# Nine tile buffers in the key and value memory, and more accumulations taken along with each chunk behind the norms

## The chip, the cores and the metric

The kernel runs as one program on one core of one Trainium2 chip. The time is device microseconds (us) of one execution; the time before is the median of three runs. TensorE (PE) multiplies, VectorE (DVE) and ScalarE (ACT) work elementwise, GpSimd (POOL) splits weights, and SyncE (SP) issues most DMA transfers.

## The reference

Two decoder layers are applied to a prompt of 1024 tokens and to 8 sequences of 4 new tokens, 1056 token columns in all, with a model width of 1024. Cut to what matters:

```python
for layer in range(2):
    h = rms_norm(x, g_attn)
    qa, ka, va, qb, kb, vb = split(h @ w_in)      # per head: rms_norm and partial rotary on q and k
    oa = dilated_attention(qa, ka, va)            # 8 heads
    ob = window_attention(qb, kb, vb, sink)       # 8 query heads, 2 key and value heads
    x = x + concat(rms_norm(oa), rms_norm(ob)) @ w_out
    h = rms_norm(x, g_ffn)
    x = x + (silu(h @ w_gate) * (h @ w_up)) @ w_down
```

The new keys and values and the moved caches are outputs too. All is float32.

## The kernel before

The activations `xm` lie transposed: 8 chunks of 128 features by 1056 tokens. Every large product is made of three TensorE matmuls on rounded parts (high by high, low by high, high by low), in the helper `product` (L402). 1056 tokens are three pieces of 352 columns (`NW`, `W`), each in a PSUM bank of its own; `ps` has eight banks. One unit of 128 output features is 3 pieces x 8 chunks x 3 matmuls = 72 matmuls of 352 columns.

**Start and end.** SP loads the input in nine tiles (`x_load`, L415) into two buffers `xy_tile`; from the third tile on it waits until TensorE has transposed the tile two before (`x_tile_turned`). VectorE copies the transposed halves into `xm` (L927). All engines meet (`met`) and the layer loop begins. After the last layer TensorE transposes back (L1658), VectorE copies two halves per tile into the same two buffers (L1280), and SP stores them; a copy into a buffer waits for the store two tiles before (`y_tile_out`).

**Norms.** A norm squares and adds the chunks, takes roots, and spreads their reciprocals over the partitions by transposes into banks 5 to 7 (`spread_roots`, L1313). Then `norm_chunks` walks over the chunks: VectorE makes chunk c (`hf`, L953), ScalarE rounds it to the high part (L689), VectorE subtracts it for the low part of chunk c-1 (L958) and signals `lo_ready`. TensorE begins the next product chunk by chunk behind that signal. Between attention and the output projection there are two norms of four chunks each; the spread of the second stands in TensorE's order behind the fourth chunk's matmuls.

**Projection.** Units are numbered u: 0 is the key of the window heads, 1 their value, then for each of four pairs p key, query, query, value (u = 2+4p to 5+4p). Units alternate between banks 0 to 2 and 3 to 5. POOL splits the weights of unit u+2 (L588, L591) once unit u is `projected`. For keys and queries ScalarE squares the unit (`head_squares`, L702), TensorE sums by heads (`sum_heads`, L1338), ScalarE takes the roots by Ln and Exp (L708, L711), VectorE applies the rotary factors (`roped`). Keys and values are turned by TensorE through banks 6 and 7 (`turn`, L1346). `stage` is one buffer: value units are copied into it to be turned (`stage_v`, L717), and turned keys are kept in it (`keep_k`, L724) until a DMA has stored them (`k_out`).

**Output projection.** `out_unit(dd, i)` is unit 2dd+i, with its weights in `f_hi[i]`, `f_lo[i]`. SP loads the weights of unit 2 only behind the second reload of `xm` (`x_back`, L544), which waits for the eighth `hf` chunk; POOL then splits them.

**Feed-forward.** A step f makes six hidden pieces (k = 0 to 5, each 48 matmuls: gate and up), and then 24 downward products of 6 matmuls. Piece k waits until piece k-2 has been multiplied by its gate (`gated`): ScalarE's Silu (L897), then VectorE's product (L1261).

The order of instructions on each engine is that of the code; nothing plans it at build time.

## Time and profile before

| what | value |
|---|---|
| median of three runs | 3042.84 us (3041.46 to 3046.21) |
| the profiled execution | 3039.55 us |
| its span | 3038.0 us |
| busy: PE, DVE, ACT, POOL | 2839.4, 1175.8, 915.5, 507.5 us |
| chain that ended last, by engine | PE 89%, DVE 5%, issue 3%, ACT 2%, DMA 1% |
| share of the chain on the product helper L402 | 68% |

The span is what the trace covers; 1.55 us of the execution lie around it. Each row of a timeline gives the start, the duration (a merged row gives the time that it covers), the engine and its line, what is written and read, the shape and the count, and in brackets the idle time before it and what ended that.

### The profile page before, as it was taken

Reading aid. Unit: us, or ns where it says so; the run is one execution under the profiler, and the core shown is the slowest. Engines: PE = TensorE matmul, PEld = TensorE weight load, DVE = VectorE, ACT = ScalarE, POOL = GpSimd, SP = SyncE. Lnnn points to the kernel's source line nnn. Section 1 sums busy time; section 2 is a strip of 40 time slices with the busy share of each in tenths; the row PEclk is TensorE's granted clock in tenths of the full one; section 3 lists DMA queues with packets and bytes.
Section 4 is the critical chain, followed back from the end, with each engine's and each line's share of the span. In section 5 each row is a group of like instructions: output and inputs, shape, how many; then the busy total and the mean of one; then the engine's idle time right before and its main releaser. Section 6 shows DMA issues by size and latency. Waiting matters only on the chain.

```text
span 3038.0 us, 51313 instructions
## 1 busy us (share of the span) xinstructions
PE 2839.4 (93%) x19000; PEld 2612.0 (86%) x19000; DVE 1175.8 (39%) x2420; ACT 915.5 (30%) x1662; POOL 507.5 (17%) x211
## 2 busy tenths in 40 slices
PE   4999899878999999999969999997889999999998
PEld 3999666578999999999959986665879999999998
DVE  5445555453322222222254455554442222322223
ACT  2334665521211111121033446654121111211110
POOL 1222000022111221122022210001212111221110
PEclk6999999978999999999979999998989999999999
DMA  4121533132555454411021244321344544454111
GB/s 160 43 63 49 169 103 104 50 99 83 182 181 181 155 175 159 153 41 52 3 94 49 63 114 130 107 77 40 99 154 159 176 153 153 153 181 140 41 41 57
DMA packets 182629, 333.35 MB, mean 110 GB/s; under 512 B 30352, under 2 KB 142096, under 8 KB 179664
## 3 DMA queue, kind: packets, MB, share of 16 engines
q1 hardware_dynamic: 171632, 195.26, 21.0%
q0 software_dynamic: 2816, 135.99, 13.4%
q8 instruction: 87, 1.43, 0.2%
q10 hardware_dynamic: 8032, 0.17, 0.2%
q14 instruction: 62, 0.51, 0.1%
HBM read 309.15 MB, written 157.94 MB: 154 GB/s over the span
## 4 chain that ended last, share of the span: by engine, by line
PE 89%; DVE 5%; issue 3%; ACT 2%; DMA 1%; DVEq 0%; ACTq 0%; SPq 0%
PE ps L402 68%; PE ps L1415 4%; PE ps L1429 3%; PE ps L1404 3%; PE ps L1338 2%; PE ps L1478 1%; DVE g_lo L958 1%; PE ps L1466 1%; PE ps L1447 1%; DVE t_buf L943 1%; PE ps L1303 1%; DVE hf L953 1%; PE ps L1454 1%; DVE hf L943 1%; DMA kt_all<-in_x_prompt_dram 1%
## 5 line engine op out<-in xcount | busy, mean ns | idle before, releaser
L402 PE MATMUL ps<-g_hi,f_hi 128*128 128x352 f32 x2496 | 816.0, 327 | 33.2 <-DVE g_lo L958 33.2
L402 PE MATMUL ps<-g_hi,f_lo 128*128 128x352 f32 x2496 | 811.9, 325 | 0.0
L402 PE MATMUL ps<-g_lo,f_hi 128*128 128x352 f32 x2496 | 810.6, 325 | 0.0
L402 PEld LDWEIGHTS ps<-g_hi,f_hi 128*128 128x128 f32 x2496 | 475.0, 190 | 39.8 <-DVE g_lo L958 39.8
L627 POOL TENSOR_TENSOR f_lo<-f_raw,f_hi 128x2048 fp32r<-128x2048 f32 x66 | 303.9, 4618 | 1197.0 <-ACT f_hi L875 1197.0
L402 PEld LDWEIGHTS ps<-g_lo,f_hi 128*128 128x128 f32 x2496 | 476.1, 191 | 0.0
L402 PEld LDWEIGHTS ps<-g_hi,f_lo 128*128 128x128 f32 x2496 | 475.9, 191 | 0.0
L1261 DVE TENSOR_TENSOR silu<-silu,ps 128x352 f32<-128x352 f32 x132 | 68.8, 521 | 821.1 <-ACT silu L897 821.1
L1271 DVE TENSOR_TENSOR xm<-xm,ps 128x352 f32<-128x352 f32 x528 | 270.9, 520 | 199.7 <-PE ps L402 199.7
L402 PE MATMUL ps<-a_hi,f_hi 128*128 128x352 f32 x1056 | 340.7, 323 | 0.0
L402 PE MATMUL ps<-a_hi,f_lo 128*128 128x352 f32 x1056 | 338.5, 321 | 0.0
L402 PE MATMUL ps<-a_lo,f_hi 128*128 128x352 f32 x1056 | 338.3, 320 | 0.0
L402 PE MATMUL ps<-h_hi,w_hi 128*128 128x352 f32 x864 | 289.6, 335 | 14.4 <-DVE h_lo L958 14.4
L402 PE MATMUL ps<-h_lo,w_hi 128*128 128x352 f32 x864 | 278.6, 323 | 0.0
L402 PE MATMUL ps<-h_hi,w_lo 128*128 128x352 f32 x864 | 278.6, 322 | 0.0
L897 ACT ACTIVATE silu<-ps 128x352 f32<-128x352 f32 x132 | 61.3, 465 | 653.5 <-PE ps L402 653.3
L763 ACT ACTIVATE pt<-ps 128x512 f32<-128x512 f32 (+3 forms) x320 | 133.4, 437 | 216.5 <-PE ps L1415 215.9
L402 PEld LDWEIGHTS ps<-a_hi,f_lo 128*128 128x128 f32 x1056 | 198.4, 188 | 0.0
L402 PEld LDWEIGHTS ps<-a_hi,f_hi 128*128 128x128 f32 x1056 | 198.1, 188 | 0.0
L402 PEld LDWEIGHTS ps<-a_lo,f_hi 128*128 128x128 f32 x1056 | 197.9, 187 | 0.0
L402 PEld LDWEIGHTS ps<-h_hi,w_hi 128*128 128x128 f32 x864 | 163.5, 189 | 20.2 <-DVE h_lo L958 17.3
L402 PEld LDWEIGHTS ps<-h_hi,w_lo 128*128 128x128 f32 x864 | 164.0, 190 | 2.8
(164 smaller groups left out, 3337.2 us busy)
## 6 DMA issues: line engine op xcount, KB each, us to landing
out_dram<-in_cache_a_dram POOLq DMA_DIRECT2D x16, 8176.0 KB, 27.1
f_raw<-in_w_gate_up_dram SPq DMA_DIRECT2D x44, 1024.0 KB, 6.3
f_raw<-in_w_down_dram SPq DMA_DIRECT2D x22, 1024.0 KB, 5.0
k_near<-in_cache_a_dram SPq DMA_DIRECT2D x16, 1024.0 KB
v_near<-in_cache_a_dram SPq DMA_DIRECT2D x16, 1024.0 KB
w_raw<-in_w_in_dram SPq DMA_DIRECT2D x28, 512.0 KB, 3.9
k_far<-in_cache_a_dram SPq DMA_DIRECT2D x16, 768.0 KB
v_far<-in_cache_a_dram SPq DMA_DIRECT2D x16, 768.0 KB
```

Of the source, the lines that this page charges most:

```text
L402: mm = pe.matmul(out, left(a, c), right(b, c), start=(start and c == 0 and k == 0), stop=(stop and c == n - 1 and k == 2))
L627: nc.gpsimd.tensor_tensor(f_lo[j][:], f_raw[j % 2][:], f_hi[j][:].bitcast(F32), ALU.subtract).then_inc(f_split.sem, 1)
L763: nc.scalar.activation(pt[:, g % 4, 0:(b - a) * P], ps[:, 3 + g % 2, 0:(b - a) * P], ACT.Copy).then_inc(pt_ready.sem, 1)
L897: nc.scalar.activation(silu[:, k % 2, :], ps[:, 2 * (k % 2), 0:W], ACT.Silu).then_inc(silued.sem, 1)
L943: nc.vector.tensor_tensor(acc[:, 0:T], acc[:, 0:T], sq[:, 0:T], ALU.add).then_inc(sq_added.sem, 1)
L953: nc.vector.scalar_tensor_tensor(hf[c % 2][:], xm[:, first + c, :], gains[:, gain + first + c:gain + first + c + 1], flat(bank), ALU.mult, ...
L1261: nc.vector.tensor_tensor(silu[:, k % 2, :], silu[:, k % 2, :], ps[:, 2 * (k % 2) + 1, 0:W], ALU.mult).then_inc(gated.sem, 1)
L1271: nc.vector.tensor_tensor(xs, xs, ps[:, 4 + (n * DC + d) % 4, 0:W], ALU.add).then_inc(ffn_added.sem, 1)
L1338: mm = pe.matmul(ps[:, bank + c, 0:W], blocks[:], t_buf[1][:, c * W:(c + 1) * W], start=True, stop=True)
L1404: pe.matmul(ps[:, k % 3, 0:w], xm[half, p + (NP if m == "b" else 0), i * P:(i + 1) * P], kt_all[half, 1 + p if m == "a" else 0, first:firs ...
L1415: mm = pe.transpose(ps[:, 3 + g % 2, (c - a) * P:(c - a + 1) * P], probs_of(d, hh)[:, c * P:(c + 1) * P], ident[:])
L1429: mm = pe.matmul(ps[half, 5, 0:P], v_all[:, 1 + p if m == "a" else 0, tiles[c], half], pt[:, g % 4, (c % 4) * P:(c % 4 + 1) * P], start=(c ...
```

## The change

1. `xy_tile` has nine buffers, made of the five key planes and four of the value planes. All nine loads are issued at once, ahead of the six constants. The waits on `x_tile_turned` in SP and on `y_tile_out` in VectorE go.
2. Behind the first norm of a layer TensorE takes with each chunk three pieces of unit 0 and two of unit 1 (15 matmuls instead of 9); unit 1's third piece follows by itself. It waits for both splits first. The order behind it changes for p = 0: the window value is staged before the roots of the window key, and turned before that key is. All banks of the units behind it are exchanged (0 to 2 with 3 to 5), and those of attention too.
3. The same behind the norms ahead of the output projection: three pieces of unit 0 and two of unit 1 with each chunk.
4. Behind the feed-forward norm the chunks take hidden pieces 0 and 1 together (12 matmuls instead of 6). Step f = 0 is written out ahead of the loop.

```diff
-        xy_tile = [kt_all[:, 2 + i, 0:SEQ] for i in range(2)]
+        xy_tile = [kt_all[:, i, 0:SEQ] for i in range(1 + NP)] + [v_all[:, i].rearrange("p j n -> p (j n)") for i in range(NP)]
@@ SP
-            x_load(0)
-            x_load(1)
+            for t in range(QT + 1):
+                x_load(t)
...
-            for t in range(2, QT + 1):
-                sp.wait_ge(x_tile_turned, 2 * (t - 1))
-                x_load(t)
@@ ACT
                 nc.scalar.activation(pieces(t_buf[1][:, 0:T]), banks(0), ACT.Square).then_inc(head_sq.sem, 1)
+                stage_v(1, 0)
                 roots_of_heads(0, 0)
-                keep_k(0, kv_rows[:, 0, NP, :])
+                keep_k(0, 2, kv_rows[:, 0, NP, :])
...
-                stage_v(1, 0)
@@ DVE, the output
-                if t >= 2:
-                    dve.wait_ge(y_tile_out[t % 2], 16 * (t // 2))
@@ PE, behind the first norm
-                pe.wait_ge(w_split.sem, w_split.at(l, 1))
+                pe.wait_ge(w_split.sem, w_split.at(l, 2))
                 for c in range(DC):
                     pe.wait_ge(lo_ready.sem, lo_ready.at(l, c + 1))
-                    for n in range(NW):
+                    for u, n in ((0, 0), (0, 1), (0, 2), (1, 0), (1, 1)):
...
-                project(1, 1, 3, (0,))
+                project(1, 1, 3, (2,))
                 sum_heads(0, 0, 0)
-                project(1, 1, 3, (1, 2))
...
                     if p == 0:
+                        pe.wait_ge(v_staged.sem, v_staged.at(l, 1))
+                        project(u, 0, 3, (0,))
+                        turn(stage, 5, v_turned)
+                        project(u, 0, 3, (1,))
+                        pe.wait_ge(v_kept.sem, v_kept.at(l, 3))
+                        project(u, 0, 3, (2,))
                         pe.wait_ge(rope.sem, rope.at(l, r))
                         turn(kt_all[:, 0, :], 2, k_turned)
+                        project(u + 1, 1, 0, (0,))
+                        sum_heads(3, h, r)
@@ PE, the output projection
-                pe.wait_ge(o_split.sem, o_split.at(l, 1))
+                pe.wait_ge(o_split.sem, o_split.at(l, 2))
                 for c in range(DC):
                     if c == NP:
                         pe.wait_ge(hf_ready.sem, hf_ready.at(l, 12))
                         spread_roots(l, 2, 5)
                     pe.wait_ge(lo_ready.sem, lo_ready.at(l, 8 + c + 1))
-                    for n in range(NW):
+                    for i, n in ((0, 0), (0, 1), (0, 2), (1, 0), (1, 1)):
...
+                product(pe, ps[:, 5, 0:W], lambda a, c: (f_hi, f_lo)[a][1][:, D + c * P:D + (c + 1) * P],
+                        lambda a, c: (g_hi, g_lo)[a][:, c, 2 * W:3 * W], DC).then_inc(o_done[1].sem, 1)
...
-                out_unit(0, 1)
@@ PE, the feed-forward
+                pe.wait_ge(f_split.sem, f_split.at(l, 2))
+                for c in range(DC):
+                    pe.wait_ge(lo_ready.sem, lo_ready.at(l, 16 + c + 1))
+                    for k in range(2):
+                        mm = hidden_chunk(k, c)
+                        if c == DC - 1:
+                            mm.then_inc(hid.sem, 1)
+                for k in range(2, HID):
+                    hidden_piece(0, k)
+                down_pieces(0)
+                with pe.Fori(1, FI) as f:
```

SP's queue at the start of the program; `kt_all` and `v_all` hold the tile buffers.

```order
 L417 DMA ident<-in_c_ident_dram 128x128
-L415 DMA kt_all<-in_x_prompt_dram 128x1024 x2
+L415 DMA kt_all<-in_x_prompt_dram 128x1024 x5
+L415 DMA v_all<-in_x_prompt_dram 128x1024 x3
+L415 DMA v_all<-in_x_sample_dram 32x1024
 L422 DMA ones<-in_c_ones_dram 128x1
 L422 DMA blocks<-in_c_blocks_dram 128x128
```

Seven of the nine loads move ahead of the constants, and nothing waits between them.

ScalarE behind the first norm of a layer, before: the squares of the key unit (L732), its roots (L708, L711), the turned key kept (L724, L727), its store, and then the value staged (L717).

```order
L732 ACTIVATE t_buf<-ps 128x1056
L707 ISA
L708 ACT_TABLE_LOAD
L708 ACTIVATE t_buf<-ps,eps 128x1056
L710 ISA
L711 ACT_TABLE_LOAD
L711 ACTIVATE t_buf<-t_buf 128x1056
```

```order
L727 ACTIVATE kv_rows<-ps 32x128
L736 ISA
L736 DMA out_dram<-stage 128x128
L715 REGISTER_ALU
L716 ISA
L717 ACTIVATE stage<-ps 128x1056
```

The same place of the changed kernel:

```order
L731 ACTIVATE t_buf<-ps 128x1056
L711 REGISTER_ALU
L714 ACTIVATE stage<-ps 128x1056
L703 ISA
L704 ACT_TABLE_LOAD
L704 ACTIVATE t_buf<-ps,eps 128x1056
```

The staging copy (L717 before, L714 now) has moved from behind the store of the kept key to behind the squares.

TensorE at the first chunk behind the feed-forward norm, before; `f_hi0` is the gate's weights and `f_hi1` those of up.

```order
L402 MATMUL ps<-g_hi,f_hi0 128x352
L402 MATMUL ps<-g_hi,f_lo0 128x352
L402 MATMUL ps<-g_lo,f_hi0 128x352
L402 MATMUL ps<-g_hi,f_hi1 128x352
L402 MATMUL ps<-g_hi,f_lo1 128x352
L402 MATMUL ps<-g_lo,f_hi1 128x352
L1634 REGISTER_ALU
```

And now, from the same place to the next chunk's wait:

```order
L1310 MATMUL ps<-ident,roots 128x32
L1663 ISA
L1665 REGISTER_ALU
L402 MATMUL ps<-g_hi,f_hi0 128x352
L402 MATMUL ps<-g_hi,f_lo0 128x352
L402 MATMUL ps<-g_lo,f_hi0 128x352
L402 MATMUL ps<-g_hi,f_hi1 128x352
L402 MATMUL ps<-g_hi,f_lo1 128x352
L402 MATMUL ps<-g_lo,f_hi1 128x352
L402 MATMUL ps<-g_hi,f_hi0 128x352
L402 MATMUL ps<-g_hi,f_lo0 128x352
L402 MATMUL ps<-g_lo,f_hi0 128x352
```

The six matmuls of piece 0 are followed by six of piece 1 (three are shown) before TensorE waits for the next chunk.

## Rows read from the trace of the kernel before

**Rows 1.** Timeline of the start of the program (start, duration, engine, operation).

```profile
10.76 3.25 ACTq L662 DMA_DIRECT2D gains_all<-in_ffn_norm_dram  x1
...
20.61 1.43 ACTq L664 DMA_DIRECT2D sinks_all<-in_sinks_b_dram  x1
...
33.56 1.28 ACT L675 ACT_TABLE_LOAD   x1 [33.56 <-DVEq L962]
```

**Rows 2.** The DMA view of the stretch from 9 to 12 us.

```profile
DMA packets 687, 1.19 MB, mean 396 GB/s; under 512 B 388, under 2 KB 407, under 8 KB 687
```

**Rows 3.** Timeline behind layer 0's first norm.

```profile
59.84 0.66 PE L402 MATMUL ps<-h_hi,w_hi 128*128 128x352 f32 x1 [3.82 <-DVE h_lo L958]
...
60.30 0.50 PE L402 MATMUL ps<-h_hi,w_lo 128*128 128x352 f32 x1
...
60.59 0.49 PE L402 MATMUL ps<-h_lo,w_hi 128*128 128x352 f32 x1
...
65.10 0.32 PE L402 MATMUL ps<-h_hi,w_hi 128*128 128x352 f32 x1
...
73.64 2.49 DVE L958 TENSOR_TENSOR h_lo<-kt_all,h_hi 128x1056 fp32r<-128x1056 f32 x2
```

**Rows 4.** The chain that ended last, in order of time (start, duration, what).

```profile
81.88 1.77 PE ps L1338 x6
...
109.93 1.77 PE ps L1338 x6
...
1603.29 1.77 PE ps L1338 x6
...
2262.79 753.89 PE ps L402 x4716
```

**Rows 5.** Timeline of TensorE behind layer 1's first norm.

```profile
1553.25 0.66 PE L402 MATMUL ps<-h_hi,w_hi 128*128 128x352 f32 x1 [3.81 <-DVE h_lo L958]
...
1556.58 0.33 PE L402 MATMUL ps<-h_lo,w_hi 128*128 128x352 f32 x1
```

**Rows 6.** Timelines of DVE, SP and POOL at layer 0's output projection.

```profile
645.54 2.54 DVE L953 SCALAR_TENSOR_TENSOR hf<-xm,gains,ps 128x1056 f32<-128x1056 f32 x2 [3.44 <-PE ps L1313]
...
669.56 1.25 DVE L1241 TENSOR_TENSOR xm<-xm,ps 128x1056 f32<-128x1056 f32 x1 [10.19 <-PE ps L402]
...
639.66 13.91 SPq L544 DMA_DIRECT2D xm<-x_spill  x2
...
664.62 2.40 POOL L591 TENSOR_TENSOR f_lo<-f_raw,f_hi 128x1024 fp32r<-128x1024 f32 x1 [0.18 <-POOL f_hi L588]
```

**Rows 7.** The same of layer 1: TensorE, POOL and VectorE.

```profile
2138.03 1.20 PE L1313 MATMUL ps<-ident,roots 128*128 128x128 f32 x9
...
2158.90 2.40 POOL L591 TENSOR_TENSOR f_lo<-f_raw,f_hi 128x1024 fp32r<-128x1024 f32 x1 [0.18 <-POOL f_hi L588]
...
2162.87 1.25 DVE L1241 TENSOR_TENSOR xm<-xm,ps 128x1056 f32<-128x1056 f32 x1 [10.34 <-PE ps L402]
```

**Rows 8.** Timelines at the first hidden pieces of both layers: TensorE's seventh chunk, ScalarE.

```profile
769.45 0.66 PE L402 MATMUL ps<-g_hi,f_hi 128*128 128x352 f32 x1 [0.39 <-DVE g_lo L958]
...
772.63 1.28 ACT L897 ACT_TABLE_LOAD   x1 [3.28 <-PE ps L402]
...
775.14 0.50 ACT L901 ACTIVATE a_hi<-silu 128x352 fp32r<-128x352 f32 x1 [0.75 <-DVE silu L1261]
...
780.23 0.46 ACT L897 ACTIVATE silu<-ps 128x352 f32<-128x352 f32 x1 [4.59 <-PE ps L402]
...
2274.28 0.46 ACT L897 ACTIVATE silu<-ps 128x352 f32<-128x352 f32 x1 [4.67 <-PE ps L402]
```

**Rows 9.** Timeline of VectorE in the output stage.

```profile
3018.36 2.48 DVE L1280 COPY kt_all<-ps 128x512 f32<-128x512 f32 x4 [1.14 <-PE ps L1658]
...
3034.30 1.28 DVE L1280 COPY kt_all<-ps 32x512 f32<-32x512 f32 x2 [1.42 <-DMA out_dram<-kt_all]
```

**Rows 10.** The DMA view from 3018 to 3024 us: GB/s in forty equal slices.

```profile
GB/s 0 0 0 0 0 109 0 0 0 0 0 0 0 0 0 0 27 410 410 437 437 410 410 410 355 383 437 437 410 410 328 410 410 437 28 0 0 0 0 0
```

More of the change, by code:

```diff
@@ L225, in trunk @@
         eps_set = sem("eps_set")
-        x_tile_in = [sem(f"x_tile_in{i}") for i in range(2)]
+        x_tile_in = [sem(f"x_tile_in{i}") for i in range(QT + 1)]
         x_tile_turned = sem("x_tile_turned")
@@ L230, in trunk @@
         y_tile_kept = sem("y_tile_kept")
-        y_tile_out = [sem(f"y_tile_out{i}") for i in range(2)]
+        y_tile_out = sem("y_tile_out")
         met = sem("met")
@@ L715, in stage_v, with keep_k @@
                     act.wait_ge(projected.sem, projected.at(l, unit + 1))
-                    act.wait_ge(k_out.sem, k_out.at(l, 16 * (n + 1)))
-                    nc.scalar.activation(pieces(stage[:]), banks(3), ACT.Copy).then_inc(v_staged.sem, 1)
-                def keep_k(n, rows):
-                    act.wait_ge(v_turned.sem, v_turned.at(l, 3 * n))
+                    if n >= 1:
+                        act.wait_ge(k_out.sem, k_out.at(l, 16 * (n + 1)))
+                    nc.scalar.activation(pieces(stage[:]), banks(0 if n else 3), ACT.Copy).then_inc(v_staged.sem, 1)
+                def keep_k(n, bank, rows):
+                    act.wait_ge(v_turned.sem, v_turned.at(l, 3 * max(n, 1)))
+                    if n == 1:
+                        act.wait_ge(k_out.sem, k_out.at(l, 16))
                     for g in range(2):
@@ L992, in roped, with k_rope @@
                     dve.wait_ge(rope.sem, rope.at(l, r + 5))
-                def k_rope(unit, gain, r, root, kt):
-                    roped(unit, 0, gain, 1.0, r, root)
+                def k_rope(unit, bank, gain, r, root, kt):
+                    roped(unit, bank, gain, 1.0, r, root)
                     nc.vector.tensor_tensor(kt, t_buf[0][:], t_buf[1][:, 0:T], ALU.mult).then_inc(rope.sem, 1)
@@ L1007, in q_rope, with keep_v @@
                                                 ALU.mult).then_inc(rope.sem, 1)
-                def keep_v(n, v, rows):
+                def keep_v(n, bank, v, rows):
                     for g in range(2):
@@ L1377, in _ @@
-                    project(u + 1, 1, 3, (1,))
-                    pe.wait_ge(v_kept.sem, v_kept.at(l, 3 * p + 3))
-                    project(u + 1, 1, 3, (2,))
+                        project(u + 1, 1, 0, (0,))
+                        sum_heads(3, h, r)
+                        project(u + 1, 1, 0, (1,))
+                        pe.wait_ge(k_kept.sem, k_kept.at(l, 3))
+                        project(u + 1, 1, 0, (2,))
+                    else:
+                        pe.wait_ge(head_root.sem, head_root.at(l, 2 * h - 1))
+                        project(u, 0, 3, (0, 1))
+                        pe.wait_ge(v_staged.sem, v_staged.at(l, p + 1))
+                        turn(stage, 2, v_turned)
+                        project(u, 0, 3, (2,))
+                        project(u + 1, 1, 0, (0,))
+                        sum_heads(3, h, r)
+                        project(u + 1, 1, 0, (1,))
+                        pe.wait_ge(v_kept.sem, v_kept.at(l, 3 * p + 3))
+                        project(u + 1, 1, 0, (2,))
@@ L1392, in _ @@
+                    project(u + 3, 1, 0, (1, 2))
                 pe.wait_ge(rope.sem, rope.at(l, K_ROPE + NP * ROPE_P))
@@ L1428, in mix @@
                             g = groups_of[d, hh][c // 4]
-                            mm = pe.matmul(ps[half, 5, 0:P], v_all[:, 1 + p if m == "a" else 0, tiles[c], half],
+                            mm = pe.matmul(ps[half, 2, 0:P], v_all[:, 1 + p if m == "a" else 0, tiles[c], half],
                                            pt[:, g % 4, (c % 4) * P:(c % 4 + 1) * P],
@@ L1650, in _ @@
                                     ).then_inc(downed.sem, 1)
+                pe.wait_ge(f_split.sem, f_split.at(l, 2))
+                for c in range(DC):
+                    pe.wait_ge(lo_ready.sem, lo_ready.at(l, 16 + c + 1))
+                    for k in range(2):
+                        mm = hidden_chunk(k, c)
+                        if c == DC - 1:
+                            mm.then_inc(hid.sem, 1)
+                for k in range(2, HID):
+                    hidden_piece(0, k)
+                down_pieces(0)
+                with pe.Fori(1, FI) as f:
+                    pe.wait_ge(f_split.sem, f_split.at(l, 3 * f + 2))
+                    for k in range(HID):
+                        hidden_piece(f, k)
+                    down_pieces(f)
                 meet(pe, l, 1)
```

116 lines of the change are left out of this document (52 added, 64 removed).

## The prediction

> **What bounds the kernel now.** The chain of waits, in order of time, comes first: apart from the norms, the start and the end it is an unbroken line of matmuls, the last of them 4716 in 753.89 us, 0.160 us each [rows 4]. Work taken off another engine is worth nothing there; TensorE has to begin work earlier in a place where it waits. Those places are read from the timelines: the start, where the layer's first instruction waits until 33.56 [rows 1]; behind each norm, where VectorE delivers a chunk every 2.51 us (first chunk 59.84, seventh at the end of the first of the two subtractions, 73.64 + 1.25 = 74.9: 15.05 over 6) [rows 3]; the output, where copies wait for stores [rows 9]. TensorE's matmuls start 0.29 us apart at first (60.30, 60.59) and last 0.32 instead of 0.50 from 65.10 on [rows 3], with starts 0.16 apart; 352 columns in 0.29 us is the 1.2 GHz level, in 0.16 about the 2.4 GHz level.
>
> **Start.** The loads of tiles 2 to 8 no longer wait for transposes and stand ahead of the constants. 4.3 MB of tiles at the 396 GB/s of [rows 2] are 11 us; begun at about 4 us, with the small gain transfers between, the last lands near 18, and two copies (about 0.65 each) per tile keep up: all is kept by 20 or 21. But the layer also waits until ScalarE has issued its gain loads. That ended at 20.61 + 1.43 = 22.0, and a single issue took 3.25 us while SP's transfers filled the engines [rows 1, 2]. SP now keeps them full to about 20 or 21 (6.2 MB), 4 or 5 us longer without a break, so I let the slow issues last 2.7 us more: 24.7. Layer start 33.4 to 24.7: **8.7 us gained**. Bounds: 12 if issuing is not slowed and the tiles decide, 3 if every issue is slow. I take 8.7, nearest to the rows.
>
> **Behind the first norm, twice.** 15 matmuls need 15 x 0.16 = 2.4 us at the upper clock, just under the chunk's 2.51; at the lower one 15 x 0.293 = 4.4. Layer 0: from 59.84 to the rise at 64.8 TensorE does 17; the other 103 follow without a gap, 16.4 us: 81.2 (never waiting, since data alone would allow 79.8). Then unit 1's last piece, 24 x 0.159 = 3.8: 85.0; summing by heads 1.77 [rows 4]: 86.8. Staging of the value runs under it (ScalarE's copy of three banks, about 1.1 from 85.1). Then unit 2's pieces 3 x 3.8, two turns of 1.2 and one piece of unit 3, 3.8: the next head sum starts at 104.5 instead of 109.93 [rows 4]: 5.5 gained. Layer 1: start 1553.25, upper clock from 1556.4 (the 0.33 of 1556.58) [rows 5], 11 done by then, 109 x 0.159: 1573.8; the same steps (23.3 us) give 1597.1 instead of 1603.29 [rows 4]: 6.2. **Together 11.7.** The second split is waited for too; TensorE's wait for the first chunk was ended by VectorE [rows 3, 5], and POOL had by then long finished both, so it costs nothing. One new tightness: the key kept in `stage`, with its store's issue, now stands right ahead of the squares of unit 2; by the same durations the squares and VectorE's first product are ready within 0.3 us of the head sum. If that cover goes, about 1 us per layer. Later pairs keep their order with other banks: zero.
>
> **Output projection, twice.** Here the gain turns round. The second norm's spread stands behind the fourth chunk's matmuls, which are now 60, not 36. In layer 0 the 24 more go at the upper clock, 3.8 us, and VectorE's fifth chunk starts at 645.54 + 3.8 [rows 6]. In layer 1 TensorE had idled 0.8 us among the four chunks before the spread at 2138.03 [rows 7], as the clock had risen sooner; that idle is filled first, and the spread comes 3.0 later, at 2141.0. The second reload of `xm` waits for the eighth chunk (the pair of issues ends at 639.66 + 13.91 = 653.57 [rows 6]), the weights of unit 2 are queued behind it on SP, and POOL's split ended at 664.62 + 2.40 = 667.0, and at 2158.90 + 2.40 = 2161.3 [rows 6, 7]. All of that moves with the spread: 670.8 and 2164.3. TensorE began unit 2 when unit 1 was done, 669.4 and 2162.7 (VectorE's additions at 669.56 and 2162.87, less 0.15) [rows 6, 7]. By its own work it would now be there at 668.9 and 2161.1: fifth chunk ready at 653.1 and 2146.1, 60 matmuls with it and the next three and 24 behind them, the first 19 and 16 of these at the lower clock. So it waits for the split: 1.4 and 1.6 later than before. **3.0 lost.** The ends: if the reload or the load behind it is quicker than before by the delay, 2.0 gained; if the lower clock holds over all of the first four chunks, 60 x 0.293 puts the spread 9 us late and the loss is 6.6 per layer.
>
> **Feed-forward norm, twice.** 12 matmuls are 1.9 us at the upper clock, so the chunks still set the pace; the backlog of the first, slow ones is caught up. Seventh chunk at 769.45 [rows 8] and 2262.79 [rows 4]; 24 x 0.159 + 0.1 for both last chunks: pieces 0 and 1 are done at 773.4 and 2266.7. But piece 2 needs piece 0 gated. Piece 0 ends 0.95 earlier, and from its end to the gate took 772.63 to 775.14, 2.5 us, with the table load of 1.28 inside, behind the wait [rows 8]. So piece 2 starts at 775.1 and 2268.4, with 1.7 us of idle TensorE where before the 48 matmuls of piece 1 hid this. Before it started at 780.1 and 2274.15 (second Silu less 0.13) [rows 8]. **5.0 + 5.8 = 10.8 gained.** If the table load were done ahead, 2.5 more; if a chunk's matmuls fell back to the lower clock near the end, 3.5 less.
>
> **Output.** The copies run free: 2.48 / 4 = 0.62 each [rows 9]. The sample tile is kept at 3018.36 + 18 x 0.64 = 3029.9 instead of 3034.30 + 1.28 = 3035.6. Stores of 0.52 MB at the 410 GB/s of the full stretches take 1.28 us each [rows 10], as long as two copies, so they trail by up to 0.5: **5.2 gained** (4.3 to 5.8). The Trainium skill has a lower limit (DMA: Bandwidth & Descriptors, "Where 436 GB/s comes from"): about 358 GB/s bind between HBM and SBUF. By it a store takes 1.46 us and eight of them end 1.4 us later, a gain of 3.8 here and a sum of 1.4 less; the rows show 410 to 437, though only for 2.6 us at a stretch, so for a long burst they leave it open.
>
> **Sum.** 8.7 + 11.7 - 3.0 + 10.8 + 5.2 = 33.4. The profiled execution took 3039.55, which gives 3006.2; the median of the runs was 3.3 above it, so 3009.5.
>
> The page on ScalarE's tables prices the switch of tables higher (the Trainium skill, ScalarE: Activation LUTs, "What ACT_TABLE_LOAD costs": about 2.66 us with a drain). Here the load is 1.28 and the Silu starts right behind it, inside the measured 2.5 [rows 8]; by the page each layer's wait would be 1.4 longer, 2.8 in all.
>
> **Rivals.**
> - *Gains at the start don't come.* The tiles arrive early, but ScalarE's issues are starved for as long as SP's transfers run: 3 instead of 8.7 gained, 3015. For it speaks the 3.25 us issue [rows 1]; against it, that most issues before it were far shorter.
> - *The projection's split is not late.* The reload's wait shifts, but the weights arrive in less time: 5 better, 3004.5. Against it stands the unbroken chain on SP [rows 6].
> - *Stores at a slower rate.* In a burst of 10 us instead of 2.6 the stores keep the 355 GB/s of a slow slice [rows 10], 1.48 us each, and the copies no longer set the pace: 1.6 less gained, 3011. For it: no stretch of full length was there before; against it: most slices show 410. (The page's limit named above would do the same.)
> - *The other side: the lower clock stays through the chunk loops.* Then every 15 matmuls take 4.4 us against 2.51, and the loops are TensorE's: 120 x 0.293 = 35.2 us instead of about 21 puts the first norm 8.3 us behind before instead of 6 ahead, per layer; the output projection loses 10 to 11 per layer, the feed-forward norm 3.5 to 4. That is 46 lost against 14 gained at start and end: 3042 + 32 = 3074. It decides if the clock does not rise in more than about half of the six loops. Against it: it rose with only 9 matmuls per chunk, within 5.0 and 3.2 us of the first one [rows 3, 5], and the loops are denser now.
> - *Not what it says:* a wait in front of an early chunk (second split, `v_staged`) cancels the overlap and the norms give nothing; start and end alone leave 3039.55 - 13.9 + 3.3 = 3029.
>
> **How the numbers follow.** Forecast 0.60, start 0.14, split not late 0.10, slower stores 0.08, overlap cancelled 0.04, clock 0.04. Each of the first four has some 4 us of its own, since the moment at which the clock rises differs between runs by about 2 us per loop. The range from 3001 to 3021 takes in those four. About 0.2% (6 us) is what a measurement here can tell. Faster 0.95, same 0.02, slower 0.03.
>
> **What would show it.** Right: the first table load near 25 us; the head sum of unit 2 20 us behind unit 0's, without idle ahead of it; VectorE's fifth chunk at the output projection 3 to 4 us later behind the first; TensorE idle ahead of unit 2, ended by POOL; 1.5 to 2 us idle ahead of piece 2, ended by VectorE; copies of the output in one run. Wrong: matmuls of 0.50 us in the second half of any chunk loop, idle of VectorE between chunks, or a layer start after 30 us.

## The result, and the profile after

The changed kernel took 3018.18 us, median of 4 runs (3009.97 to 3023.77); the kernel before 3042.40 beside it (3041.46 to 3046.21, 4 runs). The ratio is 0.9917, 95% interval 0.9904 to 0.9930: faster by 0.8%. The profiled execution is the fastest of the four, 3009.97, span 3008.4, which is 29.6 less than the 3038.0 of before. The traces are compared stage by stage, so the parts below add up to 29.6, and not to the 24 between the medians; the section on the prediction says where the difference between the two comes from.

The start. Timeline of the changed kernel, start and duration in us:

```profile
12.53 7.18 ACTq L658 DMA_DIRECT2D gains_all<-in_ffn_norm_dram  x1
...
12.79 7.23 DVE L926 COPY xm<-ps 128x512 f32<-128x512 f32 x13 [0.16 <-PE ps L1291]
...
25.76 0.53 ACTq L660 DMA_DIRECT2D sinks_all<-in_sinks_b_dram  x1
...
26.69 1.28 ACT L671 ACT_TABLE_LOAD   x1 [26.69 <-ACTq L687]
```

The tiles are kept at 12.79 + 7.23 = 20.0. The layer starts at 26.69, because ScalarE has to issue its gain loads first; one of them occupied its queue for 7.18 us. The corresponding row of before shows 3.25, and the layer began at 33.56, behind the tiles [rows 1].

Behind layer 0's first norm, timeline of the changed kernel:

```profile
52.95 0.66 PE L402 MATMUL ps<-h_hi,w_hi 128*128 128x352 f32 x1 [3.81 <-DVE h_lo L957]
...
94.88 1.05 ACT L698 ACTIVATE t_buf<-ps 128x1056 f32<-128x1056 f32 x1 [0.76 <-ACT kv_rows L726]
...
95.97 1.32 DVE L980 TENSOR_SCALAR t_buf<-ps,gains 128x1056 f32<-128x1056 f32 x1 [8.29 <-ACT t_buf L698]
...
97.34 2.04 PE L1335 MATMUL ps<-t_buf,blocks 128*128 128x352 f32 x6
```

and the head sum of unit 2 in the kernel before, in the same view:

```profile
109.77 1.94 PE L1338 MATMUL ps<-t_buf,blocks 128*128 128x352 f32 x6
```

From the first chunk's matmul to unit 2's head sum are 97.34 - 52.95 = 44.39 us; before they were 109.77 - 59.84 = 49.93 [rows 3]. (The chain in [rows 4] has that head sum 0.16 later, at 109.93, so the two views must not be mixed.) The head sum starts as soon as VectorE's product ends (95.97 + 1.32 = 97.29). That product waits for ScalarE's squares, and those wait 0.76 behind the key that ScalarE keeps (`kv_rows`).

The output projection, TensorE, POOL and SP of the changed kernel:

```profile
627.75 16.54 SPq L541 DMA_DIRECT2D xm<-x_spill  x2
...
635.02 1.20 PE L1310 MATMUL ps<-ident,roots 128*128 128x128 f32 x9
...
644.85 0.39 SPq L529 DMA_DIRECT2D f_raw<-in_w_out_dram  x1
...
654.55 1.04 POOL L584 CAST f_hi<-f_raw 128x1024 fp32r<-128x1024 f32 x1 [38.65 <-DMA f_raw<-in_w_out_dram]
...
655.76 2.35 POOL L587 TENSOR_TENSOR f_lo<-f_raw,f_hi 128x1024 fp32r<-128x1024 f32 x1 [0.18 <-POOL f_hi L584]
...
658.30 0.66 PE L402 MATMUL ps<-g_hi,f_hi 128*128 128x352 f32 x1 [3.03 <-POOL f_lo L587]
...
660.81 0.49 PE L402 MATMUL ps<-g_lo,f_hi 128*128 128x352 f32 x1
...
2143.12 0.66 PE L402 MATMUL ps<-g_hi,f_hi 128*128 128x352 f32 x1 [3.02 <-POOL f_lo L587]
```

Read it from the last wait backwards. TensorE is idle for 3.03 us in layer 0 and 3.02 in layer 1, until POOL has split unit 2's weights. POOL had waited for their load. The load was issued at 644.85, right behind the reload of `xm`, whose pair of issues ends at 627.75 + 16.54 = 644.29. Behind the wait the matmuls take 0.49 again, as at the start of a chunk loop. A window of 3 us shows it as a granted clock. Columns are the window, its length, busy time and number of instructions of PE, PEld, DVE, ACT, POOL, then the granted clock, the DMA share and GB/s. First the kernel before, which needed no wait there:

```profile
658.00:661.00 3.00, 3.00 (x21) 3.00 (x20) 1.26 (x1) 1.09 (x1) 0.00 (x0) 1.00 0.96 361
```

and the changed kernel, where the first matmuls of unit 2 ran at half clock, the 1.2 GHz level:

```profile
658.00:661.00 3.00, 2.70 (x9) 2.71 (x10) 1.23 (x1) 0.00 (x0) 2.82 (x3) 0.50 0.39 110
```

Behind the feed-forward norm, ScalarE and TensorE of the changed kernel:

```profile
762.93 1.28 ACT L896 ACT_TABLE_LOAD   x1 [3.34 <-PE ps L402]
...
765.30 0.43 PE L402 MATMUL ps<-g_hi,f_hi 128*128 128x352 f32 x1 [1.52 <-DVE silu L1260]
765.44 0.50 ACT L900 ACTIVATE a_hi<-silu 128x352 fp32r<-128x352 f32 x1 [0.75 <-DVE silu L1260]
...
773.27 0.47 ACT L896 ACTIVATE silu<-ps 128x352 f32<-128x352 f32 x1 [4.00 <-PE ps L402]
```

TensorE waits 1.52 us in front of piece 2, ended by VectorE's gate. From the table load to the kept gated piece are 765.44 - 762.93 = 2.51 us, exactly as before, 775.14 - 772.63 [rows 8]; but 48 matmuls no longer hide them.

The output, VectorE and SP of the changed kernel:

```profile
2994.44 6.07 DVE L1277 COPY kt_all<-ps 128x512 f32<-128x512 f32 x10 [1.14 <-PE ps L1685]
...
2995.76 5.12 SPq L571 DMA_DIRECT2D out_dram<-kt_all  x5
...
3000.43 4.85 DVE L1277 COPY v_all<-ps 128x512 f32<-128x512 f32 x8
...
3001.73 3.91 SPq L571 DMA_DIRECT2D out_dram<-v_all  x4
```

The copies run through, 0.61 us each, where the last one of before had waited until 3034.30 [rows 9]. The stores follow at their pace, as the DMA view from 2996 to 3008 shows (GB/s in forty slices of 0.3 us, and the sums):

```profile
GB/s 0 0 410 410 410 396 423 382 396 423 396 423 396 423 355 423 423 382 437 396 423 355 423 369 437 410 423 382 396 410 423 410 396 423 396 382 355 300 0 0
...
DMA packets 1200, 4.33 MB, mean 360 GB/s; under 512 B 144, under 2 KB 144, under 8 KB 1200
```

### The profile page after: what moved, and what is told of

Same layout as the page of the kernel before. It is cut to its first block, busy times and chain, and to the rows that moved or that the text cites. A ratio compares the mean times of both kernels' runs of the same rounds, so it can differ in the third digit from the quotient of the medians.

```text
span 3008.4 us, 51127 instructions
## 1 busy us (share of the span) xinstructions
PE 2827.9 (94%) x19000; PEld 2607.7 (87%) x19000; DVE 1171.7 (39%) x2420; ACT 916.4 (30%) x1662; POOL 510.6 (17%) x211
## 4 chain that ended last, share of the span: by engine, by line
PE 89%; DVE 4%; issue 2%; ACT 2%; ACTq 1%; DMA 1%; POOL 0%; SPq 0%; DVEq 0%; POOLq 0%
PE ps L402 69%; PE ps L1422 4%; PE ps L1436 4%; PE ps L1411 3%; PE ps L1335 2%; PE ps L1485 1%; PE ps L1473 1%; DVE g_lo L957 1%; PE ps L1454 1%; DVE t_buf L942 1%; PE ps L1300 1%; DVE hf L952 1%; PE ps L1461 1%; DVE hf L942 1%; ACT pt L762 1%
## 5 line engine op out<-in xcount | busy, mean ns | idle before, releaser
L402 PEld LDWEIGHTS ps<-g_hi,f_hi 128*128 128x128 f32 x2496 | 473.8, 190 | 38.9 <-DVE g_lo L957 28.7
L402 PEld LDWEIGHTS ps<-h_hi,w_hi 128*128 128x128 f32 x864 | 163.5, 189 | 10.8 <-DVE h_lo L957 7.9
```

The source lines that it names most:

```text
L402: mm = pe.matmul(out, left(a, c), right(b, c), start=(start and c == 0 and k == 0), stop=(stop and c == n - 1 and k == 2))
```

## The experiments

Medians are of the runs of each kernel; every ratio is to the kernel before on the same chip. The groups ran on different chips, so kernels of different groups are compared by their ratios. In the text "stretch" is the time from the output norms' first chunk to the feed-forward norm's first sum of squares in the trace of the one profiled execution: 110.4 and 109.5 us in layers 0 and 1 of the kernel before, 112.7 and 112.8 in the changed one.

| kernel | median us (range, runs) | ratio, 95% interval |
|---|---|---|
| nine buffers alone | 3033.01 (3027.77 to 3035.76, 6) | 0.9967, 0.9955 to 0.9980 |
| first norm alone | 3030.18 (3029.00 to 3031.73, 5) | 0.9964, 0.9950 to 0.9978 |
| output projection alone | 3053.17 (3046.86 to 3056.45, 7) | 1.0030, 1.0018 to 1.0041 |
| feed-forward norm alone | 3033.98 (3028.60 to 3039.34, 10) | 0.9967, 0.9957 to 0.9977 |
| changed kernel again | 3016.66 (3009.31 to 3024.25, 4) | 0.9900, 0.9877 to 0.9923 |
| all but the output projection | 3010.91 (3007.05 to 3014.16, 4) | 0.9887, 0.9869 to 0.9904 |
| weights ahead of the reloads | 3011.09 (3006.47 to 3017.64, 4) | 0.9889, 0.9867 to 0.9912 |
| that, and the wait filled | 2996.39 (2991.47 to 2998.17, 4) | 0.9836, 0.9820 to 0.9853 |
| table load ahead | 3009.39 (3008.00 to 3012.35, 4) | 0.9884, 0.9868 to 0.9901 |
| constants late | 3014.12 (3011.28 to 3020.91, 4) | 0.9902, 0.9881 to 0.9923 |
| wait filled and table ahead | 2994.45 (2993.13 to 2997.26, 4) | 0.9834, 0.9818 to 0.9851 |
| that, and constants late | 2993.96 (2991.86 to 2995.69, 4) | 0.9832, 0.9816 to 0.9849 |

The first four share 19 runs of the kernel before (median 3043.89), the next four 7 (3042.20), the last four 7 (3045.95).

### The four parts alone

Only the buffers and their waits at start and end (the parts of the diff at `xy_tile`, `x_load` and the output):

```diff
-        xy_tile = [kt_all[:, 2 + i, 0:SEQ] for i in range(2)]
+        xy_tile = [kt_all[:, i, 0:SEQ] for i in range(1 + NP)] + [v_all[:, i].rearrange("p j n -> p (j n)") for i in range(NP)]
```

> Only the nine tile buffers (all loads issued at once, no waits for stores). Theory (each part acts by itself, as the two traces show it): layer start at about 27 instead of 33.6 us, output stage 5.7 us shorter, 12.6 us faster in all; the layer start is set by ScalarE's issue of its gain loads, with single issues of 3 to 7 us. Rival (the start's gain is an accident of one execution, with ScalarE's issues free to take longer in others): 6 us or less, and the timed runs spread over more than 5 us. Rival (the spread of the changed kernel's runs, 3010 to 3024, comes from elsewhere): these runs lie within 5 us of each other, as those of before.

Measured: ratio 0.9967, about 10 us (6 to 14 by the interval). The layer starts at 26.56; in every kernel with this part and the constants in their old place it is 26.56 to 26.76, so the start is not what scatters. The six runs lie 8 us apart, and not within 5.

Only the first norm (15 matmuls per chunk and the other banks behind it):

```diff
-                    for n in range(NW):
+                    for u, n in ((0, 0), (0, 1), (0, 2), (1, 0), (1, 1)):
```

> Only 15 matmuls per chunk behind the first norm of each layer, with the new order for p = 0 and the exchanged banks. Theory: 5.7 us per layer, 11.4 faster, head sum of unit 2 at about 104.2 instead of 109.9 us. Rival (the exchanged banks cost something in attention): from the head sum of unit 2 to the end of attention more than the 495 to 498 us of before in both layers, and less than 8 us gained.

Measured: ratio 0.9964, about 11 us. From the first chunk's start on VectorE to unit 2's head sum are 48.3 and 47.9 us, against 53.7 in both layers before. The rival, a cost of the exchanged banks in attention, is not seen: from that head sum to the output norms' first chunk are 525.0 and 525.3 us, where kernels with the old banks have 522.2 to 529.1.

Only the output projection:

```diff
-                    for n in range(NW):
+                    for i, n in ((0, 0), (0, 1), (0, 2), (1, 0), (1, 1)):
```

> Only 15 matmuls per chunk behind the norms ahead of the output projection. Theory (late spread, late reload, late weights, and a fall of the clock in the wait): 5.6 us slower, TensorE idle about 3 us ahead of unit 2 with POOL as the releaser, in both layers. Rival (the part saves 36 matmuls per layer as the other norms do): 8 to 11 us faster.

Measured: ratio 1.0030 with the interval above 1, so this part alone makes the kernel slower, by 5 to 12 us. The stretch is 112.8 and 113.6. TensorE in this kernel, ahead of unit 2 in the two layers:

```profile
671.98 0.66 PE L402 MATMUL ps<-g_hi,f_hi 128*128 128x352 f32 x1 [2.80 <-POOL f_lo L591]
...
2175.92 0.43 PE L402 MATMUL ps<-g_hi,f_hi 128*128 128x352 f32 x1 [1.82 <-POOL f_lo L591]
...
2176.97 0.48 PE L402 MATMUL ps<-g_hi,f_hi 128*128 128x352 f32 x1
```

The idle of about 3 us was expected in both layers; the second had 1.82, and even that was followed by matmuls of 0.48, one microsecond later.

Only the feed-forward norm (pieces 0 and 1 taken along with every chunk):

```diff
+                for c in range(DC):
+                    pe.wait_ge(lo_ready.sem, lo_ready.at(l, 16 + c + 1))
+                    for k in range(2):
+                        mm = hidden_chunk(k, c)
```

> Only the two hidden pieces taken along behind the feed-forward norm. Theory: 5.2 and 5.9 us in the two layers, 11.1 faster, with 1.5 us of idle TensorE ahead of piece 2 ended by VectorE's gate product. Rival (the wait for the gate takes the most of it back): under 6 us.

Measured: ratio 0.9967, about 10 us, with 1.52 us of idle ahead of piece 2 in both layers. From the norm's first chunk to the third Silu are 33.8 us in both layers, against 38.7 and 39.4 before. The four ratios add up to -0.72%; for the whole change -0.83% and -1.00% were measured in two comparisons. The parts are additive within their intervals.

### Where the output projection loses

The changed kernel again, as a base for the next comparisons:

> The changed kernel once more, to stand beside the three kernels of this group. Theory (the four parts add up: 12.6 + 11.4 + 11.1 gained, about 7 lost at the output projection by the segments of the traces): 28 faster than before in the middle, single runs within about 5 us of it as in the kernel before. Rival (its runs really spread more than those of before, because the start or the clock is less steady): single runs over 10 us apart, and the profile shows where against the first one.

Measured: 0.9900, 3009.31 to 3024.25. The expectation that single runs lie within about 5 us of the middle failed: they span 15 us. The kernel before is not steady to 5 us either; its 19 runs beside the four parts span 3038.58 to 3051.95. The profiled execution here was the slowest of the four, 3024.25, which serves below to find the scatter.

The change without its output projection:

```diff
-                    for i, n in ((0, 0), (0, 1), (0, 2), (1, 0), (1, 1)):
+                    for n in range(NW):
```

> The changed kernel without its part at the output projection (9 matmuls per chunk there, unit 1 behind, as before). Theory: that part costs 3 to 4 us per layer, so this is 7 us faster than the changed kernel; from the first chunk of the output norms to the sum of the next norm 109.4 us in both layers instead of 112.8. Rival (the loss seen when the part stood alone, 9 us with an interval of 5 to 12, was that of its runs): within 3 us of the changed kernel.

Measured: 3010.91, with a stretch of 109.7 and 110.5. Without that part the changed kernel is better, 5.7 by the medians of this comparison; the ranges of runs overlap, and the traces (2.3 to 3.0 per layer) say the same.

The theory that the load of unit 2's weights is late because it is queued behind the reloads on SP. Both units' weights are issued first:

```diff
+                for i in range(2):
+                    sp.wait_ge(o_split.sem, o_split.at(l, i + 1))
+                    sp.sem_inc(waits_alone, 1)
+                    o_load(i, 2 + i)
                 for i in range(2):
                     sp.wait_ge(hf_ready.sem, hf_ready.at(l, 12 + 4 * i))
...
-                with sp.Fori(1, DC // 2) as dd:
+                with sp.Fori(2, DC // 2) as dd:
```

> The changed kernel, but SP loads the output projection's weights of units 2 and 3 ahead of both reloads of xm instead of behind them. Theory (what costs there is that the weights stand behind the late reload): TensorE's 3.0 us of idle ahead of unit 2 are gone and the clock doesn't fall, 108 us for the stretch instead of 112.8, 4.7 us per layer, 9 faster than the changed kernel. Rival (the late spread itself is what costs, or the reload is needed as early): the stretch keeps 111 us or more.

Measured: 3011.09, stretch 109.8 and 109.5, where 108 was expected. VectorE and POOL of this kernel:

```profile
643.28 2.54 DVE L956 SCALAR_TENSOR_TENSOR hf<-xm,gains,ps 128x1056 f32<-128x1056 f32 x2 [6.93 <-PE ps L1314]
...
658.69 1.04 POOL L588 CAST f_hi<-f_raw 128x1024 fp32r<-128x1024 f32 x1 [39.94 <-PE ps L402]
```

POOL now waits for TensorE to leave the old weights, and no longer for a DMA; there is no idle time ahead of unit 2. So the late split was the queue on SP. But VectorE still waits 6.93 us for the spread: the first half of the step is unchanged, and the gain of the 24 added matmuls does not arrive. TensorE of this kernel at its fifth chunk, and the window behind it:

```profile
647.06 0.66 PE L402 MATMUL ps<-g_hi,f_hi 128*128 128x352 f32 x1 [3.81 <-DVE g_lo L961]
...
645.00:652.00 7.00, 4.94 (x17) 4.94 (x18) 6.93 (x6) 3.96 (x4) 0.00 (x0) 0.53 0.09 17
```

TensorE is idle for 3.81 us there, as it was in the kernel before and in the changed one (3.8 in each layer), and the granted clock of the window is 0.53. The clock does fall in this kernel, at the fifth chunk, which the expectation of 108 had left out.

Then the same work is put where TensorE waits, behind the spread instead of in front of it:

```diff
                     if c == NP:
                         pe.wait_ge(hf_ready.sem, hf_ready.at(l, 12))
                         spread_roots(l, 2, 5)
+                        for x in range(NP):
+                            for n in range(2):
+                                out_piece(1, n, x)
                     pe.wait_ge(lo_ready.sem, lo_ready.at(l, 8 + c + 1))
                     for i, n in ((0, 0), (0, 1), (0, 2), (1, 0), (1, 1)):
+                        if i == 1 and c < NP:
+                            continue
```

> As the one before, and the second norm's spread isn't late either: with the first four chunks TensorE takes only unit 0; behind the spread, where it had idled 3.8 us for the fifth chunk, it takes unit 1's 24 matmuls of those four chunks, and with chunks five to eight all 15. Theory: another 3.8 us per layer, the stretch is 104 to 105 us, 16 us faster than the changed kernel. Rival (the lower clock eats it: the 24 matmuls run at 0.29 us and the fifth chunk waits): 107 us or more.

Measured: 2996.39, stretch 103.8 and 103.7. TensorE and VectorE of this kernel, and a window behind the spread:

```profile
637.68 1.20 PE L1314 MATMUL ps<-ident,roots 128*128 128x128 f32 x9
638.82 0.43 PE L402 MATMUL ps<-g_hi,f_hi 128*128 128x352 f32 x1
638.92 2.54 DVE L956 SCALAR_TENSOR_TENSOR hf<-xm,gains,ps 128x1056 f32<-128x1056 f32 x2 [3.08 <-PE ps L1314]
...
638.00:652.00 14.00, 14.00 (x89) 13.44 (x88) 10.07 (x9) 4.35 (x4) 0.00 (x0) 1.00 0.46 175
```

VectorE starts its fifth chunk after 3.08 us of waiting instead of 6.93, and TensorE goes on at 638.82 with unit 1's matmuls for the first four chunks, without idle. The granted clock stays at 1.00. Each layer gains 8.9 to 9.1 against the changed kernel; 2.9 to 3.3 of it are the weights, issued first, and 6.0 and 5.9 are the filled wait. That is more than the 3.8 expected for the wait alone, and the rest fits the fall of the clock behind it, which is gone as well. Against the kernel before, the output projection now gains 6.6 and 5.8 us, where the changed kernel lost 2.3 and 3.3. The filling was tried only with the weights ahead.

### The table load, the start, and all together

```diff
                 norm_hi(l, 3, hf2, g_hi)
+                nc.scalar.activation(warm[:], eps[:, 0:1], ACT.Silu)
```

A Silu of one column into a tensor of its own, so that the table is loaded ahead of the wait.

> The changed kernel with one more ScalarE instruction: a Silu of a single column into a tensor of its own, behind the last rounding of the feed-forward norm, so that the table is loaded while chunks still come. Theory (the load of 1.28 us stands inside TensorE's wait for the gate): the idle ahead of hidden piece 2 falls from 1.52 to about 0.2 us in both layers, 2.6 us in all, less than the runs' own spread can tell but plain in the profile. Rival (the wait is VectorE's and ScalarE's passes, or the table is loaded a second time at the real Silu): 1.5 us stays.

Measured: 3009.39. ScalarE and TensorE of this kernel:

```profile
760.97 1.28 ACT L892 ACT_TABLE_LOAD   x1
...
764.32 0.47 ACT L898 ACTIVATE silu<-ps 128x352 f32<-128x352 f32 x1 [1.85 <-PE ps L403]
...
765.40 0.43 PE L403 MATMUL ps<-g_hi,f_hi 128*128 128x352 f32 x1 [0.25 <-DVE silu L1262]
```

The wait in front of piece 2 shrinks from 1.52 to 0.25, and from the first chunk to the third Silu are 32.5 and 32.4 us instead of 33.7: 1.3 per layer, the length of the load. (By ratios, 0.9884 against 0.9900 and 0.9917, it is 5 to 10 us faster than the changed kernel; the intervals overlap in the one comparison and nearly in the other, and no trace ties more than 2.6 of it to the table.)

```diff
             for t in range(QT + 1):
                 x_load(t)
+            sp.wait_ge(x_tile_kept, 2 * (QT + 1))
             for dst, src in ((ones, c_ones), (blocks, c_blocks), (cos, c_cos),
                              (sin, c_sin), (mask_a, c_mask_a), (mask_b, c_mask_b)):
                 sp.dma_start(dst[:], src).then_inc(consts_in, 16)
-            sp.wait_ge(x_tile_kept, 2 * (QT + 1))
```

> The changed kernel, but SP issues the six constants only when all input tiles are kept (about 20 us) and so leaves the DMA engines free between. Theory (ScalarE's gain loads are starved while SP's transfers run, 7.2 us for one issue): that issue ends about 4 us earlier and the layer starts at 22 to 24 us instead of 26.6. Rival (the 7744 elements of the gains, moved at some 760 per us, set the time, whatever SP does): layer start at 26 us or later, or later still.

Measured: 3014.12. The start in this kernel:

```profile
12.38 4.94 ACTq L658 DMA_DIRECT2D gains_all<-in_ffn_norm_dram  x1
20.93 0.53 ACTq L660 DMA_DIRECT2D sinks_all<-in_sinks_b_dram  x1
22.57 1.75 SPq L423 DMA_DIRECT2D mask_b<-in_c_mask_b_dram  x1
24.65 1.28 ACT L671 ACT_TABLE_LOAD   x1 [24.65 <-SPq L424]
```

With less traffic from SP, ScalarE has issued everything at 21.5 instead of 26.3, so it was SP's transfers that slowed it. The gain is in two issues: the one of 7.18 ends 2.4 earlier (about 4 were expected), and the next one, which in the changed kernel lasted 3.28 us beside the constants, lasts 0.78. Now SP itself ends the wait, since it issues the constants last: the layer starts 2.0 earlier, at 24.65, and not at 22 to 24. The comparison of runs is too coarse for so small a step.

The filled wait with the table load ahead, and then the constants late as well:

> The kernel with the weights first, the wait filled behind the second norm's spread, and the table loaded ahead, all on top of the change. Theory (the parts add up): 16 + 2.6 us faster than the changed kernel, 2994 us, and faster than both. Rival (the earlier steps push the squares of a layer against GpSimd's splits, whose overlap makes VectorE's additions take 3.2 instead of 1.27 us): 2998 or more.

> As c1_all, with the constants late too. Theory: another 3 to 4 us, about 2991, if the layer start moves to 22 to 24 us. Rival (the constants now stand ahead of the first weights in SP's queue, and the second split comes too late for the first chunk): no gain, with TensorE's first chunk behind POOL instead of VectorE.

Measured: 2994.45 and 2993.96. These beat the kernel before by 1.7% and, by ratios, the changed kernel by 20 to 25 us. The sum expected of the first, 2994, came; the further 3 to 4 us of the second did not. The layer starts at 23.05 in the last of them, and TensorE's first chunk is still ended by VectorE, so its rival is not what took the gain. Its distance from the one before it (1.7 in the spans, 0.5 in the medians) is not resolved by the runs. Nor is what the table load adds to the filled wait (0.9834 against 0.9836); in the trace it is the same 1.3 per layer.

## Why the prediction was right, step by step

The forecast was 3006.2 for a profiled execution and 3009.5 for the median, range 3001 to 3021. Measured were 3009.97 and 3018.18. Direction and range held, but the median is 8.7 off, more than the 6 us that the forecast called resolvable, and the 3.8 between the profiled executions owe something to luck, as the last step shows. By its terms, spans compared:

| step | predicted | measured |
|---|---|---|
| start | 8.7 gained | 33.56 - 26.69 = 6.9 |
| first norm, twice | 11.7 | 5.54 + 5.54 = 11.1 |
| output projection, twice | 3.0 lost | 2.3 + 3.3 = 5.6 lost |
| feed-forward norm, twice | 10.8 | 4.93 + 5.63 = 10.6 |
| output | 5.2 | 19.64 - 13.96 = 5.7 |
| sum | 33.4 | 28.7, of 29.6 between the spans |

**Start.** The tiles were kept by 20.0, as forecast. The step that was mis-sized is "so I let the slow issues last 2.7 us more": ScalarE's issuing ended at 25.76 + 0.53 = 26.3, against 22.0 before, 4.3 more, and the layer began 0.4 behind that, which the forecast left out. (Its start of 33.4 should have been the 33.56 of the row.) SP's traffic lasted longer than the 20 or 21 of the forecast: the trace still shows 263 GB/s from 21 to 22 us. The experiment with late constants confirms the cause. The rival that the start gives 3 was wrong by more than my number.

**First norm.** Layer 0 came as forecast, layer 1 0.7 lower: there the clock rose 4.1 us behind the first matmul and not 3.2 as in the kernel before, about 0.5 us of work, and 0.16 is the difference between the chain's head sum and the timeline's, which the forecast mixed. The tightness that I named is there, within the 0.3 us that I gave it: the product is ready at 97.29, TensorE's last matmul ahead of the head sum starts at 96.90, and the next in a row, 0.16 later, would have been at 97.06 instead of 97.34.

**Output projection.** The order of events is the forecast one: spread late, reload late, weights late, TensorE idle, ended by POOL. The experiment with the weights ahead removed the wait and 2.9 to 3.3 per layer; by its trace the queue on SP was the cause, as argued. Its size was about half of what was measured, and one term is missing. From the first chunk on VectorE (620.07 and 2104.80; before 631.98 and 2126.25) to unit 2's first matmul, layer 0 takes 38.23 instead of 669.4 - 631.98 = 37.42, and layer 1 38.32 instead of 36.45. That is 0.8 + 1.9 = 2.7 later, against the 3.0 of the forecast (1.4 + 1.6), so the wait itself was priced rightly in its sum. (TensorE's own arrival in layer 1 should have read 2161.6 by the forecast's counts, and not 2161.1; the split at 2164.3 binds either way.) But I gave no price to what stands behind a wait. The clock fell, and the 432 matmuls from 658.30 took 70.3 us, against 68.9 for the same 432 in the kernel before: 1.4 more, and the same again in layer 1 (70.3 from 2143.12, against 68.9). 2.7 + 2.9 = 5.6, as measured. In the chunk loops I had counted every slow matmul; behind my own new wait I had not.

**Feed-forward norm.** 1.52 us idle ahead of piece 2 instead of 1.7; right within 0.3.

**Output.** The copies took 0.60 us each and gained 6.4; the stores ended 3.1 us behind the last copy instead of 2.4, which leaves 5.7. Their rate held, in slices of 355 to 437 GB/s over 11 us, 4.33 MB, about 400 on the mean. The rival of slower stores is refuted. The Trainium skill (DMA: Bandwidth & Descriptors, "Where 436 GB/s comes from") lets about 358 GB/s bind between HBM and SBUF, and the forecast took that as a lower limit for this program. The same page of the Trainium skill, where it gives its measured rates, says that about 358 is the share of each core when both cores of an HBM domain stream. Here one core runs, and its burst was not held to 358.

**Other rivals.** The clock rose in all six chunk loops, 3.3 to 5.5 us behind the first matmul, so the case of 3074 did not occur. One sign of being wrong was badly drawn: matmuls of 0.50 in the second half of a loop did come at the output projection (0.49 from 641.05 to 643.69, behind the wait of 3.81 for the fifth chunk), as the forecast's own count of slow matmuls had them there. The split that is not late is refuted by 3.03 and 3.02 of idle. The table load cost its 1.28: taking it out of the way gave 1.3 per layer, and the drain that the Trainium skill adds (ScalarE: Activation LUTs, "What ACT_TABLE_LOAD costs") is not seen here.

**From the span to the median.** "The median of the runs was 3.3 above it" failed as a step. It was a property of one sample of runs. The profiled execution of the changed kernel happened to be its fastest, 8.2 below the median; eight runs of it lie between 3009.31 and 3024.25. Two traces of the same kernel, spans 3008.4 and 3022.7, show where 14.3 us go. The feed-forward parts agree within 0.5 us per layer. The squares between attention and the output norms take 20.3 against 22.4 us in both layers, 2.1 more each; from unit 2's head sum to these squares are 3.6 and 3.1 more; the output stretches, 1.0 and 0.7 more; layer 0 up to the head sum of unit 2, 0.8. For the squares the rows tell why. VectorE and POOL in the first trace:

```profile
605.91 1.04 POOL L584 CAST f_hi<-f_raw 128x1024 fp32r<-128x1024 f32 x1 [335.38 <-DMA f_raw<-in_w_out_dram]
...
607.11 6.59 DVE L942 TENSOR_TENSOR hf<-hf,sq 128x1056 f32<-128x1056 f32 x3 [1.15 <-ACT sq L671]
607.13 3.45 POOL L587 TENSOR_TENSOR f_lo<-f_raw,f_hi 128x1024 fp32r<-128x1024 f32 x1 [0.18 <-POOL f_hi L584]
...
608.51 3.18 DVE L942 TENSOR_TENSOR hf<-hf,sq 128x1056 f32<-128x1056 f32 x1
...
610.53 2.06 POOL L584 CAST f_hi<-f_raw 128x1024 fp32r<-128x1024 f32 x1
```

and in the second:

```profile
610.10 1.13 POOL L584 CAST f_hi<-f_raw 128x1024 fp32r<-128x1024 f32 x1 [338.92 <-DMA f_raw<-in_w_out_dram]
...
611.41 2.35 POOL L587 TENSOR_TENSOR f_lo<-f_raw,f_hi 128x1024 fp32r<-128x1024 f32 x1 [0.18 <-POOL f_hi L584]
611.48 8.71 DVE L942 TENSOR_TENSOR hf<-hf,sq 128x1056 f32<-128x1056 f32 x3 [1.15 <-ACT sq L671]
611.48 3.38 DVE L942 TENSOR_TENSOR hf<-hf,sq 128x1056 f32<-128x1056 f32 x1 [1.15 <-ACT sq L671]
...
613.70 2.06 POOL L584 CAST f_hi<-f_raw 128x1024 fp32r<-128x1024 f32 x1
```

(The row of 608.51 is the second of the three additions merged at 607.11, and the row of 3.38 the first of those merged in 8.71.) By itself an addition takes 1.26 us, POOL's cast 1.04 and its subtraction 2.35. Of two that meet, the one that starts second waits for the other. In the first trace the addition starts 0.02 ahead of the subtraction; it takes 1.26, and the subtraction 3.45. In the second the subtraction starts 0.07 ahead; it takes 2.35, and the addition 3.38, ending 1.1 us behind it. From there on both engines alternate in both traces, and every later addition ends 1.1 behind a POOL instruction: the one of 608.51 at 611.70, behind the subtraction that ended at 610.58. So a few hundredths of a microsecond at one meeting decide over the 2.1 us, and the profiled execution of the changed kernel had the short case in both layers. Of the 28 such stages in the 14 traces only four are that short.

For the stages ahead of the squares the granted clock differs. Added up over the trace, the first spends about 17 us of each layer's stage at the lower level and the second about 24; at half speed 7 us more there cost about 3.5, an estimate near the 3.6 and 3.1. Over the 14 traces the stage broadly follows that sum, from 499.8 to 500.2 us where about 10 are at the lower level to 506.7 where 27 are. One place can be seen directly, the last 64 matmuls of layer 0's attention, in the first trace and in the second:

```profile
594.97:598.90 3.93, 3.93 (x64) 3.48 (x64) 2.06 (x3) 0.00 (x0) 0.00 (x0) 1.00 0.00 0
...
597.86:603.27 5.41, 5.41 (x64) 5.14 (x64) 2.07 (x3) 0.00 (x0) 0.00 (x0) 0.68 0.00 0
```

What makes the clock fall more often in one execution than in another is open: no experiment was made on it.

## What to carry to other kernels

Before work is put in front of a step, look at what stands behind it on the same engine and who waits for that: 24 matmuls ahead of a spread delayed a reload, the weights queued behind it, and with them TensorE. With the weights issued first, the same 24 behind the spread filled its wait and were worth 6 us per layer more, 9 with both edits. A wait of TensorE costs more than its length, since the matmuls behind it may start at the lower clock; price both. And one profiled execution against a median of a few runs is no fixed offset: here the median lay 3.3 us above it for the kernel before, 8.2 above it for the changed kernel, and 7.6 below it when that was run again. So small terms should be read from traces stage by stage.

## What the hardware showed that was not expected

- **The clock falls in short waits.** Behind 3.03 us of idle the granted clock was 0.50 from 658 to 661, matmuls 0.29 apart instead of 0.16; behind 3.81 us in the kernel with the weights ahead it was 0.53 from 645 to 652, and with that wait filled 1.00; behind 1.82 us in the kernel with the output part alone it fell as well, 1 us after work had begun again. A wait of 1.52 in front of piece 2 was followed by one matmul of 0.43 and then by 0.32, so there the upper level stayed.
- **Issuing a DMA can be slow for the engine that issues it.** The same gain load held ScalarE's queue for 3.25 us before, 7.18 in the changed kernel and 4.94 with the constants late, according to how long SP's transfers ran beside it. SP's tiles and then its constants count alike: the next issue, at 19.73, still took 3.28 beside the constants, and 0.78 without them. The issue at 25.76, when none of SP's transfers ran, took 0.53.
- **VectorE's additions against POOL's splits**, 1.26 to 3.38 us, as above. The Trainium skill describes such a meeting as a lock on a shared port held for the whole instruction (SBUF — State Buffer, "SBUF: two separate sides"). The traces agree: whichever starts first keeps its own time, and the record of the other includes its wait.
- **Stores from SBUF** ran at about 400 GB/s for 11 us without a break, with one core at work.
